# Query rows of the second layer's widest window group: a full fp32 product, or high and low parts stacked on the partitions

## The reference, cut to what matters

```python
def dilated_sample(q, k_ext, v_ext, dil, nback):
    B, T = q.shape[:2]
    Lb = k_ext.shape[1] - T
    idx = Lb + jnp.arange(T)[:, None] - dil * jnp.arange(nback + 1)[None, :]
    ...
    logits = jnp.einsum('bqhe,bqkhe->bhqk', q, kg).astype(jnp.float32) * (HD_D ** -0.5)
    lse = jax.nn.logsumexp(logits, axis=-1)
    p = jnp.exp(logits - lse[..., None])
    o = jnp.einsum('bhqk,bqkhe->bqhe', p.astype(v_ext.dtype), vg)
    return o, jnp.moveaxis(lse, 1, 2)
```

## Time and profile before

| | |
|---|---|
| time, median of 3 runs | 1851.21 us (1849.51 to 1853.62) |
| the profiled execution | 1850.28 us, of which its span is 1848.6 us |
| TensorE products, busy | 1793.9 us (97%) |
| TensorE weight loads, busy | 1628.3 us (88%) |
| VectorE busy | 959.4 us (52%) |
| ScalarE busy | 547.7 us (30%) |
| GpSimd busy | 158.5 us (9%) |
| transfers | 338.84 MB, mean 183 GB/s |
| granted TensorE clock, mean | 0.997 of full speed |

### The profile page before, as it was taken

The page is one execution under the profiler, slowest core; times in us unless marked ns, Lnnn a source line. Parts: engine busy times, 40 slices in busy tenths (PEclk is TensorE's granted clock), DMA queues, the critical chain, the costliest instruction groups (busy, mean ns, idle before and its releaser), DMA issues.

```text
span 1848.6 us, 36908 instructions
## 1 busy us (share of the span) xinstructions
PE 1793.9 (97%) x15099; PEld 1628.3 (88%) x15099; DVE 959.4 (52%) x1453; ACT 547.7 (30%) x1073; POOL 158.5 (9%) x210
## 2 busy tenths in 40 slices
PE   7998999999999999999999999999999999999998
PEld 6996766999999999999666768878789999999998
DVE  4336776554343534444666655467674634344344
ACT  4114556432121212322411322363223212122222
POOL 0700001210000000210000000003003000000001
PEclk9999999999999999999999999999999999999999
DMA  8229998247676776362456557733123676532221
GB/s 269 69 76 369 354 354 317 92 159 250 229 268 228 249 249 233 129 209 72 117 177 215 188 170 240 251 105 120 47 98 107 235 247 227 208 101 68 91 77 65
DMA packets 167163, 338.84 MB, mean 183 GB/s; under 512 B 9178, under 2 KB 116500, under 8 KB 165437
## 3 DMA queue, kind: packets, MB, share of 16 engines
q1 hardware_dynamic: 164691, 249.74, 40.2%
q0 software_dynamic: 2240, 87.41, 12.6%
q10 hardware_dynamic: 114, 0.03, 0.0%
HBM read 324.36 MB, written 100.19 MB: 230 GB/s over the span
## 4 chain that ended last, share of the span: by engine, by line
PE 88%; DVE 6%; ACT 2%; DMA 1%; issue 1%; SPq 1%; ACTq 0%; DVEq 0%
PE pp L665 53%; PE pp L975 16%; PE pp L1082 4%; PE pp L725 2%; PE pp L924 1%; PE pp L759 1%; PE pp L739 1%; PE pp L1129 1%; PE pp L1107 1%; PE pp L1178 1%; DMA kvring<-in_cache_b_kv 1%; ACT e_p L2160 1%; PE pp L1203 1%; PE pp L1001 1%; DVE rnorm L1320 1%
## 5 line engine op out<-in xcount | busy, mean ns | idle before, releaser
L1940 ACT ACTIVATE whi<-raw 128x1024 fp32r<-128x1024 f32 x208 | 220.6, 1061 | 958.0 <-PE pp L665 685.1
L665 PE MATMUL pp<-a_hi,whi 128*128 128x288 f32 x1280 | 275.8, 297 | 1.0 <-DVE zbuf L1333 0.7
L665 PE MATMUL pp<-a_hi,wlo 128*128 128x288 f32 x1280 | 274.5, 296 | 0.0
L665 PE MATMUL pp<-a_lo,whi 128*128 128x288 f32 x1280 | 274.5, 296 | 0.0
L1290 DVE TENSOR_TENSOR wlo<-raw,whi 128x1024 fp32r<-128x1024 f32 x208 | 255.9, 1230 | 30.7 <-ACT whi L1940 30.6
L665 PE MATMUL pp<-b_hi,whi 128*128 128x288 f32 x1152 | 246.8, 296 | 0.0
L665 PE MATMUL pp<-b_lo,whi 128*128 128x288 f32 x1152 | 246.8, 296 | 0.0
L665 PE MATMUL pp<-b_hi,wlo 128*128 128x288 f32 x1152 | 246.8, 296 | 0.0
L1349 DVE TENSOR_TENSOR x<-x,pp 128x576 f32 (+1 forms) x80 | 60.3, 754 | 292.9 <-PE pp L665 281.8
L665 PEld LDWEIGHTS pp<-a_hi,whi 128*128 128x128 f32 x1280 | 206.4, 189 | 2.3 <-issue 1.6
L665 PEld LDWEIGHTS pp<-a_hi,wlo 128*128 128x128 f32 x1280 | 206.5, 189 | 0.0
(11 more groups left out here) (300 smaller groups left out, 2112.9 us busy)
## 6 DMA issues: line engine op xcount, KB each, us to landing
kvring<-in_cache_b_kv SPq DMA_DIRECT2D x128, 512.0 KB, 5.7
out_new_d_sample<-in_cache_d_kv POOLq DMA_DIRECT2D x32, 2040.0 KB, 8.4
raw<-in_w_up SPq DMA_DIRECT2D x32, 1024.0 KB, 5.4
raw<-in_w_down SPq DMA_DIRECT2D x32, 1024.0 KB, 5.1
kring<-in_cache_d_kv SPq DMA_DIRECT2D x104, 256.0 KB, 2.8
vring<-in_cache_d_kv SPq DMA_DIRECT2D x104, 256.0 KB, 5.1
raw<-in_w_in_cd SPq DMA_DIRECT2D x24, 1024.0 KB, 5.2
out_new_d_sample<-in_cache_d_kv POOLq DMA_DIRECT2D x8, 2016.0 KB, 8.4
```

What stands on the lines that cost most here:

```text
L665: last = pe.matmul(acc_h[s][:, h, :], w[s][:, k, :], m[:, k, NH * h:NH * h + NH], start=(at_ == 0 and n == 0), stop=(at_ == KT_N - 1 and n ...
L1940: act.activation(whi_v[j], raw_v[q // 2][:, :, j, :], ACT.Copy).then_inc(whi_ready, 1)
```

## The change

The query rows are no longer kept as 64 rows of fp32. POOL first writes the query columns twice, side by side (`qdup2`), so that the four transposes give each row twice, on partitions 0 to 63 and on 64 to 127. ACT copies the upper copy to `qtok2` as fp32r (the high part) and the lower copy as fp32r to a buffer of its own (`qhi2`); DVE subtracts this from the lower copy, which leaves the low part on partitions 64 to 127 of `qtok2`. DVE also adds two halves of the identity to `both2`, 128 x 64, in which column r has a one at partitions r and 64 + r. The product in `s_query` then contracts over 128 partitions with fp32r operands, so that high and low part are added in one product. ACT's count `s1_kt_a` starts one higher (`KT_A`).

```diff
-        qtok2 = at("qtok2", W_B + 7168, 512)
+        qtok2 = at("qtok2", W_B + 7168, 512, F32R)
+        qdup2 = at("qdup2", W_B + 6144 + 512, 512)
+        qhi2, both2 = at("qhi2", W_B + 6144, 512, F32R), at("both2", W_B + 7808, NS, F32R)
...
-        KT_A = [sum(max(1, len(st[2]) // 2) for st in STEPS[16:n]) for n in range(N_ST + 1)]
+        KT_A = [1 + sum(max(1, len(st[2]) // 2) for st in STEPS[16:n]) for n in range(N_ST + 1)]
...
                 pe.wait_ge(qs_saved, 4)
                 for t in range(4):
-                    last = pe.transpose(bank[4][0:NS, P * t:P * t + P], q_s[:, 2, t, :], ident)
+                    last = pe.transpose(bank[4][:, P * t:P * t + P], qdup2[:, P * t:P * t + P], ident)
                 last.then_inc(s1_kt_ps, 1)
...
                 pe.wait_ge(s1_kt_d, max(1, j))
-                pe.matmul(bank[4 + j % 2], ident[0:NS, row:row + 1].broadcast_to([NS, P]), qtok2[0:NS, :], start=True,
+                pe.matmul(bank[4 + j % 2], both2[:, row:row + 1].broadcast_to([P, P]), qtok2[:, :], start=True,
                           stop=True).then_inc(s1_kt_ps, 1)
...
             def query_rows():
 
-                dve.wait_ge(s1_kt_ps, 1)
-                dve.tensor_copy(qtok2[0:NS, :], bank[4][0:NS, :]).then_inc(s1_kt_d, 1)
+                dve.wait_ge(s1_kt_a, 1)
+                dve.tensor_tensor(qtok2[NS:P, :], bank[4][NS:P, :], qhi2[NS:P, :].bitcast(F32), ALU.subtract)
+                dve.tensor_tensor(both2[:, :], ident[:, 0:NS], ident[:, NS:P], ALU.add).then_inc(s1_kt_d, 1)
...
             def side(i):
 
+                if i == 0:
+                    act.wait_ge(s1_kt_ps, 1)
+                    act.activation(qtok2[0:NS, :], bank[4][0:NS, :], ACT.Copy)
+                    act.activation(qhi2[NS:P, :], bank[4][NS:P, :], ACT.Copy).then_inc(s1_kt_a, 1)
...
                 pool.wait_ge(acc_free, 2 + T_CD + 12 * gi + 8)
+                if gi == 0:
+                    for r in range(2):
+                        pool.tensor_copy(qdup2[:, :].rearrange("p (t r n) -> p t r n", t=4, r=2)[:, :, r, :],
+                                         pk[:, 0:4, SEQ:N])
                 save_samples(GO[gi], 4 * gi, 12)
```

## The result

The changed kernel takes 1793.14 us (median of four runs, 1791.01 to 1795.33) against 1850.57 us, a ratio of 0.9687 (95% interval 0.9668 to 0.9706). The forecast was 1791.0 us. The profiled execution took 1794.76 us (span 1793.1 us); five more runs of the same kernel, beside the experiments, gave a median of 1793.50 us.

The account below looks back on a forecast made before the run. TensorE bounds the tiles: 64.3 us saved on query products, less 4.6 for page waits, 0.2 for the rows and 0.2 for the hand-over, gives 59.3 us off 1850.3, so 1791 us; range 1784 to 1806.

Parts of the forecast that it names:

- What bounds: Tiles with query products: TensorE, busy 97% of the span, is last, so time taken out comes off the total.
- The price of the product: Query product in TensorE's stream: 1.24 us falls to 0.236 us, saving 64.3 us over 64 products.
- both transitions: Extra spacings before and after the query product on TensorE, 0.085 and 0.1 us, vanish once neighbours are alike.
- rival B: Extra spacings around the query product stay: 0.42 us a product, saving 52 us, 1798 us; chance 0.14.
- The wait for page 2: Each tile's fourth query product waits 0.29 us for VectorE's second page, 4.6 us over 16 tiles.
- rival C: Way back from VectorE to TensorE costs 0.7 us, not 0.1: 0.89 us per tile, 1800.6 us; chance 0.09.
- VectorE's tile: VectorE's work per tile is 7.15 us before sample outputs; pages cost 1.33 us each, the split ends at 7.69.
- The rows' making: Query rows through ACT's copies, VectorE's subtraction and addition: ready at 902.65; 0.2 us allowed, between 0 and 1.
- The hand-over to the prompt attention: After tile i = 11, VectorE ends 1 us later, covered; 0.2 us for the second pair of score products.
- rival D: Transfers pace the tiles: at 256 GB/s a pair takes 20.5 us, 2.7 more, six times: 1807 us; chance 0.09.
- rival F: Value pages land late, at 13 us against 7.2 left: 70 us lost over 12 tiles, 1861 us; chance 0.02.
- Rival E: The query product still goes in four passes and costs what it costs now: 1850 us; chance 0.04.

Follow-up runs that it names:

- The third experiment: The changed kernel with each query product issued twice in a row into the same bank: 1804.26 us, ratio 0.9745 against the kernel before.
- the second experiment: The changed kernel with the single-pass query product contracting over the 64 partitions of the high part alone: 1812.41 us, ratio 0.9789 against the kernel before.
- the fourth experiment: The changed kernel with two more 256 KB HBM-to-HBM transfers in each of tiles i = 4 to 15: 1796.64 us, ratio 0.9700 against the kernel before.

## Why the prediction was right, step by step

- **What bounds:** right. TensorE stayed the last one in the tiles, and what left its stream left the total. The third experiment shows it from the other side: 0.23 us more a product, less the wait that it hides, came out at the end. Some of the nearness of the total is chance: behind the tiles the clock gave 1.6 us and took 3.1 us in the profiled execution, and neither is in the sum.
- **The price of the product:** right, 0.225 to 0.23 us for 0.236 us forecast from the pace of 288 columns. The Trainium skill's rule (page TensorE: Matmul & The Clock Gate, section Back-to-back issue gap), which the page gives for an isolated product, an estimate of 216 ns, is about as far below the measurement as the row's pace is above it.
- **Why both transitions would vanish:** right in outcome, wrong in reason and size. I priced them at 0.085 + 0.1 us from the two spacings around the product, and put them down to unlike type and height together. The two spacings were read rightly (0.1 + 0.1 us in the second experiment), but another 0.19 us lay inside the 1.06 us to the next dense product, which I read as the time of four passes. Together it is 0.39 us, and it goes with the height alone, at either type. With the prices of the prediction I put the second experiment at 1795 to 1801 us, so the mechanism was not understood: the sum came out because the new product has its neighbours' height, and all of the cost went. So rival B was mis-priced: had the transitions stayed, the product would have cost 0.62 us, not 0.42, and the total 1812 us (the second experiment), above the range that I gave. Its rows held the hint: the loader's 0.76 us of idle time ahead of the dense weights.
- **The wait for page 2:** right. 0.25 and 0.27 us in the first two tiles for 0.29, 4.5 us in all for 4.6, of which 0.35 us is a wait of the third product in tile i = 11 that I had not seen. TensorE follows VectorE's end by 0.05 us (906.29 to 906.34), so rival C fell. What I also did not see is that the product that waited delays the stream by 0.1 us more (906.34 to 906.67, 0.33 us for 0.23), and that taking the wait away would bring only half of it.
- **VectorE's tile:** pages 1.32 us apart for 1.33; the split ends 909.50 + 1.22 - 902.93 = 7.79 us after the first product, for 7.69. Tiles of 7.7 and 8.9 us were forecast as 7.6 and 8.9. The 11.34 us that I gave for i = 0 to 3 are tile 0 alone; the next two took 11.43 and 11.46 us.
- **The rows' making:** ready at 902.88 for 902.65 forecast, with a stage that ran 0.33 us late as a whole; the first product came 0.30 us after the dense pair ahead of it, where 0.265 is regular, so 0.04 us for the 0.2 allowed. POOL's two copies, 1.67 us together, end some 47 us before their reader. The hand-over to the prompt attention cost 0.2 us as forecast (4.25 us from the score products to the transposes, 4.06 before).
- **Transfers, rival D:** fell. The windows show 278 and 312 GB/s where I needed 296 over a pair, and the fourth experiment asked for more and lost 3 us.
- **Late pages, rival F:** the mechanism is there, once. A landing of 8.8 us at the longest (7.8 before), and one wait (1.81 us for TensorE, 2.1 us for its loader), which is most of the 2.3 us by which the tiles saved less than forecast (57.0 for 59.3). The forecast had left this at nothing, though its own rows had it: landings of up to 7.8 us against 7.2 us left. It differs between executions, from nothing to these 2 us.
- **Rival E:** fell; 64 records, one for each product.

Product and wait together give 64 x (1.24 - 0.2275) - 4.5 = 60.3 us, less the late page's 2 us, 58 us, against the 57.0 us of the tiles. Two terms beside these cover the last 1 us: the 0.2 us of the hand-over, and the 0.1 us behind each product that waited, 17 times.

## What to carry to other kernels

Price a TensorE product by two things that added up here: its passes, and whether its height differs from that of its neighbours. In a stream of 128-partition products a shorter one cost 0.39 us more, on 64 partitions at either type and on 8 in fp32; rows that are free can be used for something, as the low parts are here, or filled with zeros. And when a product gets cheaper by more than the consumer's pace, look at how many buffers stand between the two, and lay out one tile as a timetable: it gave the new wait to 0.04 us, though not the 0.1 us behind a product that has waited.

## What the runs showed of the hardware that was not expected

- A product on 64 partitions between products on 128 costs 0.39 us more than the same product on 128, in one pass or in four, though its weight load is no longer (182 against 185 to 192 ns); on 8 partitions, in four passes, it is 0.39 us too.
- The weight loader idles at a change of shape, of partitions (0.17 to 0.20 us) or of columns (0.17 us), and not between 24 loads of 64 partitions in a row.
- A product whose weights are loaded only as it starts, after a wait, is followed by the next dense product after 0.33 us in place of 0.23.
- Four passes of 512 columns on 128 partitions take 0.855 us of the stream, one takes 0.225 us: a pass more is 0.21 us.
- The granted clock fell to 0.50 (1.2 GHz) behind a wait of 1.82 us in one profile of the kernel and stayed at 1.00 in another, with the same instructions ahead of it; the fall cost 3.1 us.
